# Retention's sample state updates in one pass over stacked rounded and remaining rows, with their place and a gate's place in the order moved

## What is computed

```python
def retention_chunk(s_prev, q, k, v, log_g):
    c = q.shape[2]
    ...
    k_dec = k * jnp.exp(log_g[:, None] * (c - 1.0 - idx))[:, :, None]
    s_new = jnp.exp(log_g * c)[:, None, None] * s_prev + jnp.einsum('bhjd,bhje->bhde', k_dec, v)
    return s_new, o
...
ss, osm = retention_chunk(state_ret.astype(jnp.float32), qs, ks_, vs, log_g)
```

## Time and profile before

| what | value |
|---|---|
| median of 3 runs | 3501.99 us (3501.92 to 3509.51) |
| the profiled execution, its time | 3502.55 us |
| its span, first to last instruction | 3500.8 us |
| PE busy | 3339.9 us (95%) |
| DVE, ACT, POOL busy | 2123.7, 1118.6, 200.8 us |
| granted TensorE clock, mean | 0.99 |

### The profile page before, as it was taken

How to read it: one execution, slowest core, us unless ns; L and a number is a source line. 1 busy time by engine, 2 the same in 40 slices (tenths; PEclk the granted TensorE clock), 3 DMA queues, 4 the chain that set the end, 5 groups by cost and what they waited for, 6 DMA issues and landing times.

```text
span 3500.8 us, 65609 instructions
## 1 busy us (share of the span) xinstructions
PE 3339.9 (95%) x25476; PEld 2967.5 (85%) x25476; DVE 2123.7 (61%) x3225; ACT 1118.6 (32%) x1646; POOL 200.8 (6%) x157
## 2 busy tenths in 40 slices
PE   7998999999999999888999999999999999999997
PEld 7987888788788878678999999999999777777787
DVE  5466565656666666336666666766665345666655
ACT  4222232222222232214433333333332343223223
POOL 1000000000000000002000000000000222222200
PEclk9999999999999999899999999999999999999999
DMA  5466888788888888753533333333335565555534
GB/s 182 148 202 212 280 281 279 249 275 286 263 267 278 280 268 279 236 186 134 161 105 119 117 124 100 124 124 117 118 106 173 195 218 201 201 196 196 196 128 157
DMA packets 477799, 679.33 MB, mean 194 GB/s; under 512 B 32561, under 2 KB 283570, under 8 KB 474354
## 3 DMA queue, kind: packets, MB, share of 16 engines
q1 hardware_dynamic: 434882, 618.88, 53.5%
q10 hardware_dynamic: 42192, 55.98, 4.5%
q0 software_dynamic: 416, 0.28, 0.1%
HBM read 583.92 MB, written 89.52 MB: 192 GB/s over the span
## 4 chain that ended last, share of the span: by engine, by line
PE 83%; DVE 8%; issue 3%; DMA 2%; ACT 1%; SPq 1%; POOL 0%; DVEq 0%; ACTq 0%; POOLq 0%
PE low_banks L1270 56%; PE high_banks L1270 25%; PE high_banks L1273 3%; DVE WL L1902 2%; DMA area<-in_cache_v 1%; DVE area L2003 1%; SPq L1158 1%; DVE area L1988 1%; DVE area L2265 0%; ACT WH L1585 0%; DVE XL L2346 0%; DVE area L2013 0%; DMA area<-in_cache_k 0%; DMA WR<-in_w_in_ret 0%; DVE area L1976 0%
## 5 line engine op out<-in xcount | busy, mean ns | idle before, releaser
L1270 PE MATMUL low_banks<-XH,WH 128*128 128x288 f32 (+2 forms) x4632 | 1126.4, 310 | 36.0 <-DVE WL L1902 11.6
L1270 PE MATMUL low_banks<-XH,WL 128*128 128x288 f32 (+2 forms) x4632 | 1062.8, 297 | 0.0
L1270 PE MATMUL low_banks<-XL,WH 128*128 128x288 f32 (+2 forms) x4632 | 1060.9, 296 | 0.0
L1270 PEld LDWEIGHTS low_banks<-XH,WH 128*128 128x128 f32 x4632 | 769.3, 190 | 171.9 <-issue 139.5
L1270 PEld LDWEIGHTS low_banks<-XL,WH 128*128 128x128 f32 x4632 | 772.5, 190 | 0.0
L1270 PEld LDWEIGHTS low_banks<-XH,WL 128*128 128x128 f32 x4632 | 771.6, 189 | 0.0
L1270 PE MATMUL high_banks<-area 128*32 128x256 f32 (+7 forms) x4912 | 610.9, 456 | 34.8 <-DMA area<-in_cache_v 16.2
L1270 PEld LDWEIGHTS high_banks<-area 128*32 128x32 f32 (+3 forms) x4912 | 274.0, 139 | 244.8 <-issue 177.3
L1585 ACT ACTIVATE WH<-WR 128x1024 fp32r<-128x1024 f32 x272 | 287.4, 1057 | 545.5 <-PE low_banks L1270 453.6
L1902 DVE TENSOR_TENSOR WL<-WR,WH 128x1024 fp32r<-128x1024 f32 x272 | 343.7, 1264 | 131.2 <-ACT WH L1585 125.6
L2003 DVE STREAM_TRANSPOSE area<-area 128x512 f32<-128x512 f32 x512 | 335.1, 691 | 111.5 <-PE high_banks L1270 59.3
(11 more groups left out here) (184 smaller groups left out, 3260.7 us busy)
## 6 DMA issues: line engine op xcount, KB each, us to landing
area<-in_cache_k SPq DMA_DIRECT2D x512, 256.0 KB, 4.8
area<-in_cache_v SPq DMA_DIRECT2D x512, 256.0 KB, 5.3
area<-in_w_in_ret SPq DMA_DIRECT2D x162, 512.0 KB, 5.7
WR<-in_w_in_attn SPq DMA_DIRECT2D x136, 512.0 KB, 5.4
WR<-in_w_out_ret SPq DMA_DIRECT2D x66, 512.0 KB, 3.8
area<-in_state_ret SPq DMA_DIRECT2D x64, 512.0 KB, 7.5
out<-area SPq DMA_DIRECT2D x64, 512.0 KB, 5.4
WR<-in_w_in_ret SPq DMA_DIRECT2D x38, 512.0 KB, 4.0
```

Source lines behind the costliest of these rows:

```text
L1270: return nc.tensor.matmul(out, a, b, start=start, stop=stop, skip_group_check=True)
```

## The change

Key and value rows of the sample sequences are put three times into a 32-row group, and split: for eight rows k and v the group holds, in this order, rounded k, remaining k, rounded k, and rounded v, rounded v, remaining v (the last eight rows are zero). One fp32r matmul then gives the three products that matter. The rows come by DMA: values eight times 32 rows from the DRAM copy (`load_v3`, at 4), keys first to a DRAM buffer (`store_k`, at 10) and from there in eight DMAs (`load_k3`, at 13). ACT rounds and scales, DVE combines (`pad_v` at 16, `pad_k` at 20). `v3` lies in the tiles 2 and 3 of `oN`, free between heads. `rs_state` goes from 24+9c to 23+9c, and the gate of tile 4 from 51 to 55.

```diff
-        kz = np.where((r % 32 < 2 * NQ)[:, None] & ((r % 32 // NQ)[:, None] == np.arange(2)[None]),
-                      np.exp(lg * (NQ - 1.0 - r % NQ))[:, None], 0) * w
+        third = r % 32 // NQ
+        fade = np.where(third < 3, np.exp(lg * (NQ - 1.0 - r % NQ)), 0) * w
+        kz = np.stack([fade, fade * (third == 1), np.array([1.0, -1, 1, 0])[third], third == 2, np.array([1.0, 1, -1, 0])[third]], 1)
...
-    put(10, Stage("pad_rows"))
-    put(17, Stage("rs_mask"))
+    put(4, Stage("load_v3"))
+    put(10, Stage("store_k"))
+    put(13, Stage("load_k3"))
+    put(16, Stage("pad_v"))
+    put(20, Stage("pad_k"))
...
-        put(24 + 9 * c - (c == 3), Stage("rs_state", g_=c // 2, e=c % 2))
+        put(23 + 9 * c - (c == 3), Stage("rs_state", g_=c // 2, e=c % 2))
...
-    put(51, Stage("gate", t=4, norm=norms[4]))
+    put(55, Stage("gate", t=4, norm=norms[4]))
...
+            def thrice(to, rows):
+                per = rows.rearrange("(j g i) n -> j g i n", g=2, i=NQ)
+                for j, n in itertools.product(range(4), range(2)):
+                    yield to[32 * j:32 * j + 32, n, :], per[j, n].rearrange("(o i) n -> o i n", o=1).broadcast_to([4, NQ, rows.shape[1]])
...
+            def store_k(g):
                 sp.wait_ge(sem["drained5"], c.before("drained5"))
+                sp.wait_ge(sem["k3_in"], c.before("k3_in"))
+                sp.dma_start(keys_d, kn_s[:]).then_inc(sem["k_out"], 16)
...
-                    mm(bank[4 + j][:, :], kz[rows, g_, e * 128:(e + 1) * 128], rvz[rows, :]).then_inc(sem[f"full{4 + j}"], 1)
+                    mm(bank[4 + j][:, :], kz[rows, g_, e * 128:(e + 1) * 128], vz[rows, g_, :]).then_inc(sem[f"full{4 + j}"], 1)
...
+            def pad_k(g):
+                act.wait_ge(sem["k3_in"], c.before("k3_in"))
+                copy(kz, k3, scale=hc[:, 384:385])
+                copy(k3, k3, scale=hc[:, 385:386]).then_inc(sem["pad_hi"], 1)
...
+            def pad_k(g):
+                dve.wait_ge(sem["pad_hi"], c.done("pad_hi"))
+                v.scalar_tensor_tensor(out=kz, in0=kz.bitcast(f32), scalar=hc[:, 386:387], in1=k3, op0=MUL, op1=ADD).then_inc(sem["kz_ready"], 1)
```

More of the change, by code:

```diff
@@ L1776, in rs_keys, with pad_v @@
                 act.wait_ge(sem["full5"], c.done("full5"))
-                act.wait_ge(sem["padded_in"], c.before("padded_in"))
+                act.wait_ge(sem["k_out"], c.before("k_out"))
                 copy(kn_s[:], bank[5][0:SMP, 0:256]).then_inc(sem["drained5"], 1)
+            def pad_v(g):
+                act.wait_ge(sem["v3_in"], c.before("v3_in"))
+                act.wait_ge(sem["head_in"], c.before("head_in"))
+                for n in range(4, 8):
+                    act.wait_ge(sem[f"full{n}"], c.before(f"full{n}"))
+                copy(vz, v3)
+                copy(v3, v3, scale=hc[:, 387:388]).then_inc(sem["pad_hi"], 1)
+            def pad_k(g):
+                act.wait_ge(sem["k3_in"], c.before("k3_in"))
+                copy(kz, k3, scale=hc[:, 384:385])
+                copy(k3, k3, scale=hc[:, 385:386]).then_inc(sem["pad_hi"], 1)
             def ret_scores(g, c_):
                 act.wait_ge(sem["full5"], c.done("full5"))
-                copy(kd[:], bank[5][:, 0:256], scale=hc[:, 386:387]).then_inc(sem["drained5"], 1)
+                copy(kd[:], bank[5][:, 0:256], scale=hc[:, 389:390]).then_inc(sem["drained5"], 1)
             def square(c_):
@@ L2224, in rs_keys, with pad_v @@
                                 hc[0:SMP, 320:384].rearrange("p (j r) -> p j r", r=16), MUL).then_inc(sem["drained4"], 1)
-            def rs_mask(g):
-                dve.wait_ge(sem["padded_in"], c.before("padded_in"))
-                for n in range(4, 8):
-                    dve.wait_ge(sem[f"full{n}"], c.before(f"full{n}"))
-                for b_ in range(2):
-                    ins = v.tensor_scalar(kz[:, b_, :], knz[:], hc[:, 384 + b_:385 + b_], None, MUL)
-                    if b_:
-                        ins.then_inc(sem["kz_ready"], 1)
-                    else:
-                        o.link(ins)
+            def pad_v(g):
+                dve.wait_ge(sem["pad_hi"], c.done("pad_hi"))
+                v.scalar_tensor_tensor(out=vz, in0=vz.bitcast(f32), scalar=hc[:, 388:389], in1=v3, op0=MUL, op1=ADD).then_inc(sem["kz_ready"], 1)
+            def pad_k(g):
+                dve.wait_ge(sem["pad_hi"], c.done("pad_hi"))
+                v.scalar_tensor_tensor(out=kz, in0=kz.bitcast(f32), scalar=hc[:, 386:387], in1=k3, op0=MUL, op1=ADD).then_inc(sem["kz_ready"], 1)
             def ret_scores(g, c_):
@@ L2248, in ret_state @@
                     if c_:
[L2249 removed]
+                        ins = v.scalar_tensor_tensor(out=Sp[:, e, :], in0=Sp[:, e, :], scalar=hc[:, 390:391], in1=bank[4 + e][:, :],
                                                      op0=MUL, op1=ADD)
```

49 lines of the change are left out of this document (27 added, 22 removed).

## The result

| | before | after |
|---|---|---|
| median (lowest to highest), us | 3502.24 (3501.92 to 3509.51) | 3527.12 (3526.09 to 3532.77) |
| ratio to before, 95% interval | 1 | 1.0068 (1.0054 to 1.0083) |
| profiled execution, us | 3502.55 | 3527.88 |
| its span, us | 3500.8 | 3526.1 |

What follows compares the result with a forecast made beforehand. PE was taken to bound the kernel (83% of the chain). Update -5.0, new order +21.7, gate -13.4, weight split -2.6, clock -1.7 and row preparation 0 sum to -1.0: about 3501 us, range 3487 to 3524.

Steps and rivals of the forecast that it cites:

- with 1.4 on ACT and 0.75 on DVE 3063.9 ... 3.3 us to spare, price 0: Keys' chain in each head: prepared keys ready at 3063.9, PE wants them at 3067.2; price 0, upper bound 38 us.
- so `rs_out` should not wait: Loading part of a head: the last of eight state loads goes out sooner than before, so no wait for states.
- the middle: Keys' 64 KB store: 5.4 us to landing, between 2.7 at the least and 8.1 behind a large load.
- Rival 1: SyncE's queue: keys late, or repeated-source transfers slow and holding it up; 24 us, about 3525; chance 0.20.
- The rule on the number of engines: Stacked-row loads: a source repeated four times would use four DMA engines; 0 to 16 us more.
- The clock: Around the first head's 4.16 us wait: without it the granted clock no longer falls there; -1.7 us.
- Rival 2: Update with c = 0: PE's idle gap of 1.7 us lowers the clock in up to six heads; +10, about 3511; chance 0.06.
- the mechanism of the update's cost: Updates c = 0 to 2: scores right behind wait for DVE's drain, hiding the faster matmul; +21.7 us together.
- The order's cost and the pass: Three updates of four: new order costs +21.7 us; at the old place the saved pass is worth 15 more.
- sum of -1: Whole kernel: all terms together make -1.0 us, the parts nearly cancelling; about 3501 us for the median.
- the gate: Gate of tile 4, moved four steps later: eight waits (-10.7) and most of the 4.16 us wait (-2.7) go; -13.4 us.
- the split behind it: Weight split behind the gate: starts sooner, ahead of the long GpSimd instruction, so PE's waits in three heads go; -2.6 us.

Runs made afterwards that it cites:

- plain: Changed kernel with the 16 stacked-row transfers of a head reading 32 consecutive rows, so new sample states are wrong: 3504.7 us, 1.0002 of the kernel before.
- b_rs23: Kernel before with the three state updates per head that have a scores step right behind them one step sooner: 3516.0 us, 1.0037 of the kernel before.
- order24_k4: Changed kernel with updates back at 24+9c, keys stored repeated and reloaded from plain rows, values still with repeated source: 3502.9 us, 0.9999 of the kernel before.
- float_pass: Changed kernel with its state-update matmuls read as float32, so in two passes: 3532.2 us, 1.0077 of the kernel before.
- order24_plain: Changed kernel with updates back at 24+9c and stacked-row transfers reading 32 consecutive rows (new sample states wrong): 3472.7 us, 0.9909 of the kernel before.
- b_gate55: Kernel before with the gate of tile 4 moved from 51 to 55: 3495.1 us, 0.9974 of the kernel before.
- order24_spread: Changed kernel with updates back at 24+9c, keys and values stored repeated and reloaded from 32 consecutive rows: 3482.6 us, 0.9943 of the kernel before.
- order24: Changed kernel with its state updates back at their old place, 24+9c: 3490.8 us, 0.9966 of the kernel before.
- spread23: Changed kernel, its order kept, with keys and values stored repeated and reloaded from 32 consecutive rows: 3515.3 us, 1.0036 of the kernel before.

## Why the prediction was wrong

**The step that failed** is "with 1.4 on ACT and 0.75 on DVE 3063.9 ... 3.3 us to spare, price 0", together with "so `rs_out` should not wait". Taken apart on the chain of the keys in the head at 3140 us:

- From the keys' copy to the store: forecast 0.8, measured 3.0. The values' issues were counted, but as having passed; they had not, at 0.65 each, and two states' issues stood behind them.
- The store: forecast 5.4, "the middle", measured 7.85, and 7.8 in the median of six. It lay within the bounds, but the middle had no row behind it. The earlier trace rows had a small load behind large ones at 8.1, which is the nearer case. The repeated source has no part in this term: plain has 8.1.
- The reload: 7 x 0.6 + 2.7 forecast, 4.6 + 3.8 measured.

Together 6.1 us more, against 3.3 to spare. **Rival 1** names this and has the time almost to the us (about 3525), with the cause it named second: transfers with a repeated source, slower than plain ones, hold up the queue. That its number fits is in part luck. It came from 8 x 3 us of PE waiting for the keys; what PE waits for ScalarE, behind the keys, is 4.0 us in four. The larger part of PE's new waits is for the states in the same queue, 12.1 us in six, and the rest is the clock's. For the states the failed step is the reason given: the last one does go out sooner than before, 8.0 instead of 5.7 us ahead of its use, but it lands after 9.3 instead of 4.4. On ScalarE the keys hold up squares and a rounding, which PE wants first.

**The rule on the number of engines**, from the Trainium skill, gave 0 to 16 us. Plain sources take 23 off; the direction was right, and the chance given to it too low. Whether few engines or the longer issue make the transfers slow stays open.

**The clock** was -1.7, the rows say up to 17 us the other way. Rival 2 had +10 at 0.06. Its argument against itself, that a gap of 1.34 had left the clock up, held for that gap and for those of b_rs23, and not for 1.44 and more, at c = 1 as well as at c = 0. The runs with the one kind of gap and with the other (plain, order24_k4) show 0.98 each. In plain, where no transfer is waited for, that is up to 11 us, which is rival 2's price.

**Right**: the mechanism of the update's cost. The forecast had the scores' and transposes' starts to within 0.06 us, and the pass is hidden in three updates of four (float_pass). **Right in part by luck**: its sum. The order's cost and the pass were forecast as 37 us together and measured 36, 33 and 33 in three pairs. But the kernels with the new order are at 0.98 or 0.97 of the clock and order24_plain at 1.00, and in the pair plain and order24_plain up to 11 of the 33 are the clock's, which the forecast did not have there. So the waits alone cost less than forecast; at the old place PE waits for other things, as in order24_plain 7.7 us for x_rows, where plain has 3.3.

The plain kernel, 1.0002 of the kernel before or 5 us longer by its stretch, is near the sum of -1 for the same reason: some 11 for the clock and 7 to 10 for a gate worth less stand against an order and a pass that cost less than forecast. The terms cancel, they were not all right.

**Mis-sized**: the gate. 13.4 were forecast for it and 2.6 for the split behind it, 6 to 9 measured for the move by the medians, 0.5 to 6 by the stretches. In the kernel before the wait for the split grew where the gate's went (b_gate55). In the changed kernel it did vanish, and part of the gate's waits would have shrunk without the move, as b_rs23 shows.

The waits of the kernel after don't add up exactly. 16.4 us for states and ScalarE and up to 17 for the clock are 33 beside a sum of -1, so 32; the stretch has 28.9 and the medians 25. The clock's 17 is an upper bound, since PE partly waits at the low level as well, and the rest stays open.

## What to carry to other kernels

- Before a buffer's reader is moved ahead of its neighbour, ask who drains the buffer it fills. A faster matmul in front of a fixed drain is worth nothing; behind other work the same matmul is worth all it saves. Here one step in the order decided over 33 to 36 us, more than the new computation.
- A load that repeats rows by a stride of zero isn't priced by its bytes: the same bytes from plain rows were 23 us cheaper here (plain). Storing rows repeated and reading them plain was 8 us faster here than reading them repeated (order24_spread against order24, intervals that touch), in the changed order 11 us (spread23 against after), and with the old order the change is a gain of 20.
- A queue in order passes its lateness to whatever stands behind: price a new transfer at the latest state load and at the engine whose next instruction is queued behind the consumer, not only at its own reader.

## What the runs showed of the hardware

- Issuing a transfer with a fourfold repeated source holds SyncE's queue for 0.61 us in the median, one of 32 consecutive rows for 0.42 (plain); eight take 5.22 and 3.64 us with the gaps between them.
- Four row groups' fp32r matmuls of 512 columns take 0.51 us side by side, two-pass float32 ones 1.14.
- A 64 KB store lands after 7.8 us in the median here, as late as a load of 512 KB beside it (8.1), the queue ahead being the same:

```profile
area<-in_state_ret SPq DMA_DIRECT2D x43, 512.0 KB, 8.1
...
retention_sample_keys<-area SPq DMA_DIRECT2D x6, 64.0 KB, 7.8
```

- Waits of 0.92 to 1.02 us, 18 of them, left the granted clock at 1.00 from 2880 to 3440 us (b_rs23). With waits of 1.66 and 1.45 and late loads it was 0.97, with the waits alone (plain) 0.98, in six falls of which two stand behind a wait of 1.44 or 1.45.
